# Recurrent heads with the input gate added in exponents, and another order of the first group: a two-layer hybrid decoder step on one Trainium2 core

## What is computed

```python
log_f = jnp.logaddexp(jnp.log(lb), jnp.log1p(-lb) + jax.nn.log_sigmoid(fl))
k_in = (1.0 - lb) * jax.nn.sigmoid(-fl)
...
G = jnp.cumsum(lc, axis=2)                       # lc: log_f of a chunk
A = jnp.einsum('bhtd,bhsd,bhtsd->bhts', qc, kc, decay)      # decay = exp(G_t - G_s), s <= t
o = jnp.einsum('bhts,bhse->bhte', A, vc) + jnp.einsum('bhtd,bhde->bhte', qc * jnp.exp(G), S)
S = jnp.exp(Gl)[..., None] * S + jnp.einsum('bhsd,bhse->bhde', kc * jnp.exp(Gl[:, :, None] - G), vc)
```

## Time and profile before

| what | value |
|---|---|
| time, median of 3 runs | 1358.71 us (1358.7 to 1358.9) |
| the profiled execution, its own time | 1358.26 us |
| its span, first to last instruction | 1356.5 us |
| TensorE matmuls busy | 1323.3 us (98%) |
| VectorE busy | 817.7 us (60%) |
| ScalarE busy | 602.5 us (44%) |
| GpSimd busy | 233.6 us (17%) |
| granted TensorE clock, mean | 0.994 of full |
| chain of waits that ended last: TensorE, VectorE, ScalarE | 78%, 10%, 5% |

### The profile page before, as it was taken

The page is one execution under the profiler, slowest core; times in us unless marked ns, Lnnn a source line. Parts: engine busy times, 40 slices in busy tenths (PEclk is TensorE's granted clock), DMA queues, the critical chain, the costliest instruction groups (busy, mean ns, idle before and its releaser), DMA issues.

```text
span 1356.5 us, 30303 instructions
## 1 busy us (share of the span) xinstructions
PE 1323.3 (98%) x11820; PEld 1290.5 (95%) x11820; DVE 817.7 (60%) x1401; ACT 602.5 (44%) x1230; POOL 233.6 (17%) x365
## 2 busy tenths in 40 slices
PE   8999999999999999997999999999999999999997
PEld 8998999999999999996999999989999999999996
DVE  6476576656565622248888888867566555552224
ACT  5366355433333322236666666655533333332221
POOL 3111121111111100001322222211111111120000
PEclk9999999999999999999999999999999999999999
DMA  7311231323222332213323232322122222332211
GB/s 272 116 60 63 81 94 48 94 89 93 89 81 91 108 104 89 74 49 92 111 95 95 95 95 95 95 96 94 40 94 85 87 83 93 99 119 87 86 43 66
DMA packets 39683, 123.39 MB, mean 91 GB/s; under 512 B 4232, under 2 KB 12040, under 8 KB 39496
## 3 DMA queue, kind: packets, MB, share of 16 engines
q1 hardware_dynamic: 35400, 111.92, 26.1%
q10 hardware_dynamic: 4048, 10.20, 2.2%
q0 software_dynamic: 176, 0.44, 0.1%
HBM read 113.98 MB, written 8.57 MB: 90 GB/s over the span
## 4 chain that ended last, share of the span: by engine, by line
PE 78%; DVE 10%; ACT 5%; issue 4%; POOL 1%; DMA 0%; ACTq 0%; DVEq 0%; SPq 0%; POOLq 0%
PE acc L428 74%; DVE w_lo L1310 1%; ACT w_hi L846 1%; DVE lev L1661 1%; DVE x L1516 1%; ACT Snew L1262 1%; DVE mix L1511 1%; DVE Snew L1792 1%; DVE scratch L1778 1%; DVE AT L1728 1%; PE aux L587 0%; DVE lev L1667 0%; ACT AT L1224 0%; DMA x<-in_xT 0%; DVE h_lo L1319 0%
## 5 line engine op out<-in xcount | busy, mean ns | idle before, releaser
L1310 DVE TENSOR_TENSOR w_lo<-raw,w_hi 128x512 fp32r<-128x512 f32 (+1 forms) x372 | 306.4, 827 | 335.0 <-ACT w_hi L846 334.6
L428 PE MATMUL acc<-h_hi,w_hi 128*128 128x272 f32 x2208 | 477.2, 294 | 7.1 <-DVE w_lo L1310 2.3
L428 PE MATMUL acc<-h_hi,w_lo 128*128 128x272 f32 x2208 | 465.3, 289 | 0.0
L428 PE MATMUL acc<-h_lo,w_hi 128*128 128x272 f32 x2208 | 464.0, 288 | 0.0
L428 PEld LDWEIGHTS acc<-h_hi,w_hi 128*128 128x128 f32 x2208 | 350.7, 189 | 18.4 <-issue 7.4
L846 ACT CAST w_hi<-raw 128x512 fp32r<-128x512 f32 (+1 forms) x372 | 236.5, 642 | 267.2 <-PE acc L428 262.2
L428 PEld LDWEIGHTS acc<-h_lo,w_hi 128*128 128x128 f32 x2208 | 350.8, 189 | 0.2
L428 PEld LDWEIGHTS acc<-h_hi,w_lo 128*128 128x128 f32 x2208 | 348.7, 189 | 0.0
L428 PE MATMUL acc<-g_hi,w_hi 128*128 128x272 f32 x704 | 153.1, 288 | 0.0
L428 PE MATMUL acc<-g_hi,w_lo 128*128 128x272 f32 x704 | 153.0, 289 | 0.0
L428 PE MATMUL acc<-g_lo,w_hi 128*128 128x272 f32 x704 | 152.4, 288 | 0.0
(11 more groups left out here) (247 smaller groups left out, 1418.8 us busy)
## 6 DMA issues: line engine op xcount, KB each, us to landing
raw<-in_w_up SPq DMA_DIRECT2D x88, 512.0 KB, 3.5
raw<-in_w_down SPq DMA_DIRECT2D x32, 704.0 KB, 4.1
raw<-in_w_in_c SPq DMA_DIRECT2D x32, 512.0 KB, 3.6
raw<-in_w_in_ab SPq DMA_DIRECT2D x18, 512.0 KB, 3.7
raw<-in_w_out_ab SPq DMA_DIRECT2D x8, 512.0 KB, 3.5
S<-in_state ACTq DMA_DIRECT2D x8, 512.0 KB, 3.6
o_ss<-Snew ACTq DMA_DIRECT2D x8, 512.0 KB, 2.7
raw<-in_w_out_c SPq DMA_DIRECT2D x8, 512.0 KB, 3.5
```

The costliest lines, as they stand in the source:

```text
L428: mm = pe.matmul(acc[out][:, t, 0:H], w[slot][:, wc], mv[:, kk_, t * H:(t + 1) * H], start=start and k == 0 and q == 0, stop=stop and k == ...
L1310: dve.tensor_tensor(w_lo[slot][:, to], raw[n % 4][:, cols], w_hi[slot][:, to], ALU.subtract).then_inc(lo_ready, 1)
```

## The change

It has three parts. (1) First group: x tile 1 is issued on the SP queue between the weights of units 0 and 1; TensorE takes tiles 0 and 1 of unit 0 and then tiles 0 and 1 of unit 1; ScalarE's squares of tiles 0 and 1 come after the `h_hi` of tile 2, each later one a round later than before; VectorE adds the squares, GpSimd none. (2) Heads: `ln k_in` is taken into the exponent. `Gk = G - ln k_in` is one more add, and it stands in for `G` wherever `kk` was multiplied in, so that those products fall away: on GpSimd one over `kd` and four over `lev`, on VectorE the one over `E2`. `E1` and `E2` now have subtractions of their own, and a level has two, of 256 columns. One small logarithm and one small maximum prepare `ln(1 - lb)`. (3) The state adds of `prev` come first in tick 3, ahead of `c_qn`, and `diag_ops` follows `kd_ops` at once.

```diff
 @block.sync
-                        if u == 1:
-                            for k in range(1, KD):
-                                sp_q.dma_start(x[:, k, :], dram["xT"][:, k, :]).then_inc(x_in[k], 16)
+                        for k in {0: (1,), 1: range(2, KD)}.get(u, ()):
+                            sp_q.dma_start(x[:, k, :], dram["xT"][:, k, :]).then_inc(x_in[k], 16)
 @block.tensor
-                    for k in range(8):
+                    for k, u in [(0, 0), (1, 0), (0, 1), (1, 1)] + [(k, u) for k in range(2, 8) for u in range(2)]:
...
-                        pe.wait_ge(C["diag_ready"], 2 * prev + 2)
+                        pe.wait_ge(C["diag_ready"], prev + 1)
+                        pe.wait_ge(C["diag_exp"], 2 * prev + 2)
...
-                        pe.wait_ge(C["lev_ready"], 8 * prev + 8)
+                        pe.wait_ge(C["lev_ready"], 4 * prev + 4)
 @block.scalar
-                buffer_free(0, k)
-                act.activation(S[k % 2][:], x[:, k, :], ACT.Square).then_inc(sq_ready, 1)
+                for s in {0: (), 1: (), 2: (0, 1)}.get(k, (k - 1, k) if k == 7 else (k - 1,)):
+                    buffer_free(0, s)
+                    act.activation(S[s % 2][:], x[:, s, :], ACT.Square).then_inc(sq_ready, 1)
...
+                if post == 1:
+                    act.wait_ge(C["lb_ready"], 2)
+                    act.activation(lb[:, 4, :], lb[:, 3, :], ACT.Ln).then_inc(C["lb_done"], 1)
...
-                        act.activation(kd[:], kd[:], ACT.Exp).then_inc(C["kd_exp"], 1)
+                        act.activation(kd[:], kd[:], ACT.Exp).then_inc(C["kd_ready"], 1)
...
-                        act.activation(E1[:], E2[:], ACT.Exp)
+                        act.activation(E1[:], E1[:], ACT.Exp).then_inc(C["diag_exp"], 1)
 @block.vector
+            def square_added(k):
+
+                dve.wait_ge(sq_ready, k + 1)
+                if k == 1:
+                    dve.tensor_tensor(S[2][:], S[0][:], S[1][:], ALU.add).then_inc(sq_added, 2)
+                else:
+                    dve.wait_ge(sq_added, k)
+                    dve.tensor_tensor(S[2][:], S[2][:], S[k % 2][:], ALU.add).then_inc(sq_added, 1)
...
+                if k >= 2:
+                    square_added(k - 1)
...
-                dve.tensor_tensor(v, g, mid, ALU.subtract).then_inc(C["lev_diff"], 1)
+                dve.tensor_tensor(v[:, :, 0, :], gk[:, :, 0, :], mid, ALU.subtract)
+                dve.tensor_tensor(v[:, :, 1, :], g[:, :, 1, :], mid, ALU.subtract).then_inc(C["lev_diff"], 1)
...
+            def state_added(prev):
+
+                dve.wait_ge(C["s0_scaled"], prev + 1)
+                for z in range(2):
+                    dve.wait_ge(C["us_done"], 2 * prev + 1 + z)
+                    half_b = slice(4 * z, 4 * z + 4)
+                    dve.tensor_tensor(Snew[:, half_b, :], Snew[:, half_b, :],
+                                      A[z][:].rearrange("p (a b) -> p a b", a=4), ALU.add).then_inc(C["snew_ready"], 1)
+
             def kd_ops(cur):
 
                 dve.wait_ge(C["G_ready"], cur + 1)
+                step.mark(dve.tensor_tensor(Gk[:], G[:], S[0][:], ALU.add))
+                step.wait(dve)
...
             def diag_ops(cur):
...
+                for to, of in ((E1, G), (E2, Gk)):
+                    dve.tensor_tensor(to[:, 0:TP].rearrange("p (c s) -> p c s", s=8),
+                                      of[:, 0:TP].rearrange("p (c s) -> p c s", s=8),
+                                      g8[:, :, 3:4].broadcast_to([P, TP // 8, 8]), ALU.subtract)
+                    i_ = dve.tensor_tensor(sample(to[:, TP:T]), sample(of[:, TP:T]),
+                                           gs_[:, :, 1:2].broadcast_to([P, NB, TS]), ALU.subtract)
...
+                    if t == 3:
+                        dve.wait_ge(C["qG_ready"], cur)
...
-                    dve.scalar_tensor_tensor(kk[:], S[0][:], one_lb, S[1][:], ALU.mult, ALU.mult)
-                    step.mark(dve.tensor_scalar(S[1][:], S[1][:], one_lb, low, ALU.mult, ALU.add))
+                    dve.scalar_tensor_tensor(S[0][:], S[0][:], ln_one_lb, S[1][:], ALU.subtract, ALU.add)
+                    step.mark(dve.tensor_scalar(Gk[:], Gk[:], one_lb, low, ALU.mult, ALU.add))
...
-                    dve.wait_ge(C["diag_exp"], cur + 1)
-                    dve.tensor_tensor(E2[:], E2[:], kk[:], ALU.mult).then_inc(C["diag_ready"], 1)
...
+                    if t == 3 and prev is not None:
+                        state_added(prev)
 @block.gpsimd
-            add_squares(0)
...
-                    pool.wait_ge(C["kd_exp"], cur + 1)
-                    pool.tensor_tensor(kd[:], kd[:], kk[:], ALU.mult).then_inc(C["kd_ready"], 1)
...
-                pool.wait_ge(C["lev_exp"], 4 * cur + l + 1)
-                v, k_ = [z.rearrange("p (n a s) -> p n a s", a=2, s=SPANS[l]) for z in (lev[l][:], kk[:, 0:TP])]
-                pool.tensor_tensor(v[:, :, 0, :], v[:, :, 0, :], k_[:, :, 0, :], ALU.mult).then_inc(C["lev_ready"], 1)
```

More of the change, by code:

```diff
@@ L460, in first_pair @@
                 if norm == 0:
-                    for k in range(8):
+                    for k, u in [(0, 0), (1, 0), (0, 1), (1, 1)] + [(k, u) for k in range(2, 8) for u in range(2)]:
                         e = k // 4
-                        for u in range(2):
-                            half(m + 2 * u + e, 0, u, h, 4 * e, e == 0, e == 1, tile_ready(0) if u == 0 else None,
-                                 ks=[k % 4], signal={(0, 3): 1, (0, 7): 1, (1, 7): 2}.get((u, k), 0))
+                        half(m + 2 * u + e, 0, u, h, 4 * e, e == 0, e == 1, tile_ready(0) if u == 0 else None,
+                             ks=[k % 4], signal={(0, 3): 1, (0, 7): 1, (1, 7): 2}.get((u, k), 0))
                     for t in range(2):
@@ L1787, in hgrn_tick @@
                         kd_ops(cur)
-                    dve.wait_ge(C["s0_scaled"], prev + 1)
-                    for z in range(2):
-                        dve.wait_ge(C["us_done"], 2 * prev + 1 + z)
-                        half_b = slice(4 * z, 4 * z + 4)
-                        dve.tensor_tensor(Snew[:, half_b, :], Snew[:, half_b, :],
-                                          A[z][:].rearrange("p (a b) -> p a b", a=4), ALU.add).then_inc(C["snew_ready"], 1)
-                    if cur is not None:
                         diag_ops(cur)
+                    else:
+                        state_added(prev)
                 if cur is None:
@@ L1847, in _ @@
             head(0, None, 0)
-            base, STEPS_C = step.n, 4
+            base, STEPS_C = step.n, 5
             with dve.Fori(1, HEADS - 1) as hd:
@@ L1967, in hgrn @@
                     pool.wait_ge(evac, tile("in_c", 1) + 4 * cur)
-                    pool.wait_ge(C["diag_exp"], cur + 1)
+                    pool.wait_ge(C["diag_exp"], 2 * cur + 1)
                     pool.tensor_tensor(E1[:], E1[:], qn[:], ALU.mult).then_inc(C["diag_ready"], 1)
-                    for l in range(4):
-                        key_level(l, cur)
-                        if l == 0:
-                            if prev is not None:
-                                pool.wait_ge(C["oc_done"], prev + 1)
-                            pool.wait_ge(C["eG_ready"], cur + 1)
-                            pool.tensor_tensor(qG[:], eG[:], qn[:], ALU.mult).then_inc(C["qG_ready"], 1)
-            def key_level(l, cur):
-                pool.wait_ge(C["lev_exp"], 4 * cur + l + 1)
-                v, k_ = [z.rearrange("p (n a s) -> p n a s", a=2, s=SPANS[l]) for z in (lev[l][:], kk[:, 0:TP])]
-                pool.tensor_tensor(v[:, :, 0, :], v[:, :, 0, :], k_[:, :, 0, :], ALU.mult).then_inc(C["lev_ready"], 1)
+                    if prev is not None:
+                        pool.wait_ge(C["oc_done"], prev + 1)
+                    pool.wait_ge(C["eG_ready"], cur + 1)
+                    pool.tensor_tensor(qG[:], eG[:], qn[:], ALU.mult).then_inc(C["qG_ready"], 1)
             pool.wait_ge(half_done, 2 * UNIT0["in_c"])
```

40 lines of the change are left out of this document (21 added, 19 removed).

## The result

The changed kernel takes **1351.06 us** (median of 5 runs, 1350.48 to 1351.98), against 1358.7 before (5 runs on the same chip, 1357.68 to 1358.9). The ratio is 0.9943, 95% interval 0.9933 to 0.9954: 7.6 us faster, where 5.0 were forecast and the range ended at 1351.5.

The account below looks back on a forecast made before the run. TensorE, busy 98% of the span, was taken as the bound. First group - 3.0, state adds - 1.6, head 0 + 0.4, last head - 0.8 sum to - 5.0: 1358.7 to 1353.7 us, range 1351.5 to 1356.3.

Parts of the forecast that it names:

- First group, - 3.0: Start of the kernel: TensorE's first matmuls end at 20.3 instead of 23.25, 3.0 us gained if the clock holds.
- State adds first, - 1.6: Tick 3 of the heads: six TensorE waits for the state adds vanish, 1.6 us gained, and work delayed behind them stays hidden.
- Gate, heads 1 to 7: Input gate in exponents: VectorE's work falls 0.8 us a head, TensorE covers it, so no gain was summed here.
- Head 0, + 0.4: In head 0, L781 (transposes of `kd`) gains 0.6 us, but L788 (transposes of `vv`) comes 0.4 later: 0.4 us lost.
- The 1.1 us that the levels lose to GpSimd stay, since its product over `E1` falls on them still: Head 0, on the chain to `vv`: GpSimd's product still slows VectorE's two level subtractions by 1.1 us, as before.
- the bound of 1.7 more: Slow-clock stretch in head 0: its 1.5 us loss was left unchanged, with bounds of 0.5 less and 1.7 more.
- Last head, - 0.8: End of the last head: of two TensorE waits of 0.7 us, 0.8 is gained, bounds 0 and 1.6; ScalarE's later copies oppose.
- A level split: Each level's subtraction written as two of 256 columns: 0.1 us more on VectorE, bounds 0 and 0.45.
- The clock did not fall at 10.0: Rival for the start of the kernel: the clock falls at 10.0 all the same, gain 1.5 instead of 3.0, 1355.2; chance 0.15.
- the first group gave its all: Rival: the start gives almost nothing, as x tile 1 lands late and VectorE becomes its bound, 1356.5; chance 0.07.
- ScalarE's root: Rival: in heads 1 to 7 the norm's root queues behind `kd`'s exponents, delaying L781; 1357.2 or slower; chances 0.04 and 0.04.
- Heads gain more: Rival: VectorE's relief shortens the chain to `vv` and the slow stretch behind shrinks, 1 to 2 us more, 1352.2; chance 0.13.

Follow-up runs that it names:

- part 1 alone: The kernel before with only the first group's edits (x tile 1 sooner, TensorE's order, later squares, adds on VectorE): 1356.88 us.
- The last experiment: The changed kernel with spare matmuls in head 0, and head 6's state adds, in the last head's tick 3, back in their old place: 1349.90 us.
- parts 2 and 3 alone: The kernel before with the input gate in exponents and the state adds first, its first group unchanged: 1354.71 us.

## Why the prediction was wrong

The sign and the places were right, and so were the mechanisms of the first group. Two steps failed: the size and the independence of the state adds' waits in heads 1 to 7, and the hold of the levels by GpSimd in head 0. The sum was 2.2 us of span too small (5.0 for 7.2): 0.2 in the first group, 0.7 in head 0, 1.0 in the other heads, 0.3 in the last. The medians, which differ by 7.6, add 0.4.

- **First group, - 3.0: right.** 3.22 by the first norm's sum, 3.10 with part 1 alone. The order on the three engines, the clock and the cost of an add (0.72 for 0.71) came as worked out. Tile 1 of x landed no later than worked out (6.5): its `h_hi` starts at 6.41. Weights came later than I took (8.03, not 7.75). The argument for the clock, twice the work in the stretch ahead, is not shown to be the criterion, since it was kept once after 1.35 and fell after 1.69. "Half of the gain" for the clock was not seen in the new order, where it never fell; in the old order, with the adds beside `h_lo`, a kept clock gave nothing.
- **State adds first, - 1.6: the step "Six waits are 1.6 us" failed, in its size and in what it assumes.** In size: from TensorE's last listed pair of matmuls before L771 (734.55) to L771 (735.23) there are 0.68 us from start to start, where matmuls without a wait stand 0.25 apart, so the wait costs 0.43 and not the 0.26 listed; taken away, it gave 0.43 (6.77 to 6.34), and 0.1 more behind the sum. The listed idle time begins where the modelled end of a pipelined matmul lies, and is short by the difference. In what it assumes: that no other wait stands right behind, "so both are hidden". They were not; alone the edit gave 0.05 a head, since TensorE then waited 0.27 more at L706 and 0.17 more at L750.
- **Gate, heads 1 to 7: the sum has no term for it, and that failed.** The prediction asks what TensorE needs in ticks 4 and 5, where VectorE is behind; about L706 and L750, which stand in ticks 0 to 3, it does not ask outside the last head. VectorE's busy time fell from 86.5 to 82.4 in three heads, 1.4 a head (I had worked out 0.8, with 0.3 for four splits that at 0.1 each are 0.4), and with it the 0.27 of waiting for `AT_s` that the state adds first bring when alone. Together the period fell by 0.41, which from head 1's norm sum to head 7's is 2.64 where 1.6 was forecast: 1.0 of the missing 2.2. By the table of groups this is about 0.55 a head at the norm's sum, where 0.27 was taken, less 0.12 that TensorE now waits more at L750.
- **Head 0, + 0.4: failed, the measured effect is - 0.3.** L781 was right (0.68 sooner for 0.6). The step that failed is "The 1.1 us that the levels lose to GpSimd stay, since its product over `E1` falls on them still". It fell on them and did not hold them: VectorE had begun its first level at 635.70, 0.34 ahead of GpSimd's product, and kept going; the product waited for the run to end (2.29 less 1.37 alone is 0.92). In the kernel before, and with the levels in halves alone, GpSimd had begun first, by 0.11 and 0.12, and VectorE was held. From L781 to L788 it takes 3.29 in the changed kernel, 3.52 before, and the forecast comes to 4.5. The page "SBUF — State Buffer" of the Trainium skill (SBUF: two separate sides) says that of a VectorE instruction with two inputs in SBUF and a GpSimd instruction the first to start has their shared port pair for its whole instruction, and that the other is blocked; the rows agree, and show besides that GpSimd got it only after VectorE's four instructions, each 0.33 behind the last. So L788 came 0.9 sooner after the shift by 3.2, not 0.4 later. Of this 0.6 went back: the clock was 0.50 until 642.1, over 4.29 us of TensorE's work instead of 2.96, a loss of 2.1 and not the 1.5 that I left as it was; the bound of 1.7 more held. Net, 0.7 of the missing 2.2.
- **Last head, - 0.8: right in size (- 1.06), by another balance, so in part by luck.** From head 7's `kd` on the gate gives 2.05 and the state adds first take back 1.1 through ScalarE's `v_s`, the counter-effect that I had named at up to 1. The last experiment shows that it isn't won back by order.
- **A level split:** 0.1 taken, 0.06 measured by VectorE's busy time. On its own it made the period 0.12 longer; in the changed kernel VectorE loses more work than the splits add.
- **The rivals.** The clock did not fall at 10.0, the first group gave its all, and ScalarE's root did not become the limit, though it was close: 0.7 us more on VectorE made it so. "Heads gain more" is what came, with its reason half right: GpSimd's product did begin later than the levels and the chain to `vv` did get shorter; the slow stretch behind it did not, more of TensorE's work lay in it. Its 0.13 was too little, and its 1352.2 still too small.

What is not settled: that the waits at L706 and L750 stand behind VectorE and ScalarE was read from timelines and not tried by an edit of its own; how much of the 1.4 us of VectorE's relief is contention and how much fewer instructions was not told apart, since no kernel had a spare GpSimd product in the place of the removed ones; and what decides whether the clock falls at 10.0 or in head 0 stays open.

## What to carry to other kernels

A wait on the list of the busiest engine is worth its length only if nothing else stands within that length behind it. Take its length from start to start of the matmuls and not from the list. In a loop a removed wait comes back at the next place where the busiest engine needs the others: two edits can give almost nothing alone and the gain together. Cut the period at fixed places in each kernel, and see which piece shrinks and which grows. For moved work, see which of VectorE and GpSimd starts first at the new place, and what the freed queue starts sooner: a product moved off GpSimd let the next one fall on the one subtraction on the critical path. And look at the granted clock of each profiled execution before you read a difference of 1 or 2 us as the edit's.

## What the runs showed of the hardware

- The same pair of engines, VectorE and GpSimd, hold each other by turns: 0.69 to 1.70 and 0.41 to 1.55 for VectorE's instruction where GpSimd began first, 1.37 to 2.29 for GpSimd's where VectorE did. Moving an instruction away moves the hold to another: with the state adds first, the subtraction for `c_E` fell from 1.55 to 0.68, and `w_lo` rose from 0.71 to 0.82 in the mean of 40, and VectorE's busy time stayed at 86.5 in three heads (86.49 and 86.56).
- The slow stretch of head 0 began and ended at other places in each kernel, with nearly the same waits there: 638.06 to 644.89 before, about 635.2 to 642.1 after, about 636.4 to 646.6 with parts 2 and 3 alone. From the transposes of `vv` to head 1's norm sum, with the same code, it took 25.15 with the clock at 1.00 throughout, 27.05 in the changed kernel and 27.85 with parts 2 and 3 alone. A gain ahead of such a stretch can't be priced to better than 1 us from the trace of before.
- Twelve matmuls of work that nobody reads, put into two waits, were worth 2.0 us at once and 1.5 at the end in one profiled execution; in two more kernels with the same twelve the clock was 0.50 for part of head 0 all the same.
